# Three more raw slots for expert pieces, and a branch on TensorE that chooses between two programs that run to the end of a transformer kernel

## What is computed

```python
x = x + short_conv_mixer(rmsnorm(x), ...)            # conv
x = x + swiglu(rmsnorm(x), ...)                      # ffn1
x = x + mla_mixer(rmsnorm(x), ...)                   # mla, 8 heads
x = x + moe_swiglu(rmsnorm(x), router, ...)          # moe, 8 experts, 2 per token

x = x + fox_and_pool(rmsnorm(x), ...) @ w_out        # fox, 8 heads
x = x + memory_attention(rmsnorm(x), mem, ...)       # mem, 4 heads
x = x + swiglu(rmsnorm(x), ...)                      # ffn2
```

```python
probs = jax.nn.softmax(ht @ router)
vals, idx = lax.top_k(probs, 2)
gates = ...                                           # vals normalised, scattered to 8 columns
for e in range(8):
    out = out + gates[:, e:e + 1] * swiglu(ht, w_gate[e], w_up[e], w_down[e])
```

## Time and profile before

| | us |
|---|---|
| median of 3 runs (1244.38 to 1245.68) | 1245.11 |
| the profiled execution | 1246.09 |
| its span, first to last instruction | 1244.2 |
| TensorE busy in it | 1200.9 (97%) |
| bytes read from HBM in it | 326.26 MB |
| mean granted TensorE clock | 0.994 |

### The profile page before, as it was taken

How to read it: one execution, slowest core, us unless ns; L and a number is a source line. 1 busy time by engine, 2 the same in 40 slices (tenths; PEclk the granted TensorE clock), 3 DMA queues, 4 the chain that set the end, 5 groups by cost and what they waited for, 6 DMA issues and landing times.

```text
span 1244.2 us, 18366 instructions
## 1 busy us (share of the span) xinstructions
PE 1200.9 (97%) x7857; PEld 811.2 (65%) x7857; DVE 479.8 (39%) x710; ACT 450.0 (36%) x695; POOL 28.6 (2%) x49
## 2 busy tenths in 40 slices
PE   7999999999999999999999999988999998999998
PEld 6887888888877354436434443433688876888886
DVE  4686545546675410001001000002666664655542
ACT  6646444335775101000101100011676656444431
POOL 4000000000000000000000000010100000000000
PEclk9999999999999999999999999989999999999999
DMA  9745655553447989999999999999952450755540
GB/s 308 253 137 203 203 177 181 184 160 126 154 153 278 416 348 400 422 421 419 422 421 421 420 421 421 420 419 381 356 203 102 136 168 1 262 178 190 182 135 35
DMA packets 88019, 330.89 MB, mean 266 GB/s; under 512 B 5995, under 2 KB 13888, under 8 KB 64384
## 3 DMA queue, kind: packets, MB, share of 16 engines
q1 hardware_dynamic: 85040, 322.35, 68.3%
q0 software_dynamic: 2736, 7.27, 1.7%
q10 hardware_dynamic: 160, 0.07, 0.0%
HBM read 326.26 MB, written 3.41 MB: 265 GB/s over the span
## 4 chain that ended last, share of the span: by engine, by line
PE 86%; DMA 7%; DVE 3%; ACT 3%; issue 1%; SPq 0%; ACTq 0%; DVEq 0%
PE bank L1756 16%; PE bank L1758 16%; PE bank L1757 16%; PE bank L2108 11%; PE bank L2114 7%; PE bank L2167 7%; PE bank L2184 2%; DMA raw_beside<-in_moe_w_up 2%; DMA back<-in_moe_w_gate 2%; PE bank L2090 2%; DMA raw_over_lo<-in_moe_w_up 2%; PE bank L2204 1%; DVE w_lo L411 1%; PE bank L1851 1%; PE bank L1868 1%
## 5 line engine op out<-in xcount | busy, mean ns | idle before, releaser
L411 DVE TENSOR_TENSOR w_lo<-raw,w_hi 128x2048 fp32r<-128x2048 f32 (+3 forms) x118 | 258.0, 2200 | 169.3 <-ACT w_hi L406 169.1
L406 ACT ACTIVATE w_hi<-raw 128x2048 fp32r<-128x2048 f32 (+3 forms) x118 | 216.3, 1843 | 164.8 <-PE bank L1758 160.4
L1756 PE MATMUL bank<-w_hi,xT_hi 128*128 128x512 f32 (+2 forms) x672 | 256.8, 382 | 3.0 <-issue 1.5
L1757 PE MATMUL bank<-w_lo,xT_hi 128*128 128x512 f32 (+2 forms) x672 | 253.5, 377 | 0.0
L1758 PE MATMUL bank<-w_hi,xT_lo 128*128 128x512 f32 (+2 forms) x672 | 253.4, 377 | 0.0
L1497 DVE TENSOR_TENSOR e_act<-bank,e_act 128x512 f32<-128x512 f32 x20 | 13.8, 692 | 353.6 <-PE bank L2108 190.9
L1756 PEld LDWEIGHTS bank<-w_hi,xT_hi 128*128 128x128 f32 x672 | 127.1, 189 | 27.1 <-issue 3.7
L1758 PEld LDWEIGHTS bank<-w_hi,xT_lo 128*128 128x128 f32 x672 | 127.0, 189 | 23.0
L1757 PEld LDWEIGHTS bank<-w_lo,xT_hi 128*128 128x128 f32 x672 | 127.1, 189 | 21.7
L890 ACT ACTIVATE eT<-bank 128x512 f32<-128x512 f32 x20 | 11.5, 596 | 165.2 <-PE bank L2147 165.2
L1756 PE MATMUL bank<-w_hi,ffn_hi 128*128 128x512 f32 x176 | 68.7, 390 | 0.0
(11 more groups left out here) (428 smaller groups left out, 1415.1 us busy)
## 6 DMA issues: line engine op xcount, KB each, us to landing
raw<-in_w_gate_up SPq DMA_DIRECT2D x22, 1024.0 KB, 5.2
raw<-in_moe_w_down SPq DMA_DIRECT2D x18, 1024.0 KB, 22.1
raw_over_hi<-in_moe_w_up SPq DMA_DIRECT2D x17, 1024.0 KB, 23.4
raw_over_lo<-in_moe_w_up SPq DMA_DIRECT2D x17, 1024.0 KB, 24.2
raw<-in_moe_w_gate SPq DMA_DIRECT2D x16, 1024.0 KB, 22.0
raw_over_hi<-in_moe_w_gate SPq DMA_DIRECT2D x16, 1024.0 KB, 21.3
raw_over_lo<-in_moe_w_gate SPq DMA_DIRECT2D x16, 1024.0 KB, 22.1
raw_over_hi<-in_moe_w_down SPq DMA_DIRECT2D x16, 1024.0 KB, 19.8
```

The costliest lines, as they stand in the source:

```text
L406: nc.scalar.activation(w_hi[:, slot, :n], raw[:, slot, :n], ACT.Copy).then_inc(stream.high, 1)
L411: nc.vector.tensor_tensor(w_lo[:, slot, :n], raw[:, slot, :n], w_hi[:, slot, :n].bitcast(F32), ALU.subtract).then_inc(stream.low, 1)
L1756: mm(dst, a_hi, b_hi, start=start, stop=False)
L1757: mm(dst, a_hi, b_lo, start=False, stop=False)
```

## The change

**Slots.** EXPERT_RING becomes 19. The three new slots are a tile raw_more of 3 MB at the end of the moe region of SBUF. Room for it is made by taking two tiles out of the region: y now lies in the memory of junk (the scratch output of the squares of a norm), and moe_g, the norm's gain, in that of e_act. Piece n takes slot n % 19, and LAST_SLOTS is written anew. The first owners of the new slots (pieces 16, 17 and 18) wait for moe_product, as pieces 14 and 15 do. TensorE's use of piece n releases the issue of piece n + 19.

**Branch.** What TensorE does from the last expert to the end of the kernel becomes a function finish(over), called in both arms of a branch: finish(0) where there is no overflow, and the rounds followed by finish(1) where there is. The other engines keep their code.

```diff
-EXPERT_RING = 16
+EXPERT_RING = 19
-LAST_SLOTS = (*range(8, 16), *range(2, 8), 8, 9, 10, 11, 3, 4, 8, 9, 10, 11)
+LAST_SLOTS = (*range(16, 19), *range(2, 16), *range(16, 19), 6, 7, 8, 9)
...
+        with ExitStack() as inner:
+            y_in_junk = inner.enter_context(nc.sbuf_tensor("y_in_junk", [P, D], F32))
         junk = sb("junk", [P, T, D], mybir.dt.bfloat16)
...
-        region(back=[P, 2 * T, D], moe_g=[P, D], y=[P, D], h=[P, T, D],
+        region(back=[P, 2 * T, D], h=[P, T, D],
...
-               ahead_of=[P, T, E, E], least=[P, E, E], load=[P, 12, E])
+               ahead_of=[P, T, E, E], least=[P, E, E], load=[P, 12, E],
+               raw_more=[P, EXPERT_RING - 16, CHUNK])
+        M["y"] = y_in_junk
+        M["moe_g"] = M["e_act"][:, :, :].rearrange("p g n -> p (g n)")[:, :D]
...
-            return views + [raw_beside[:, s, :] for s in range(2)]
+            return views + [raw_beside[:, s, :] for s in range(2)] + [M["raw_more"][:, s, :] for s in range(EXPERT_RING - 16)]
...
-                pe.wait_ge(sem("moe_planned"), 1)
-                over = pe.value_load(overflow[0:1, 0:1], min_val=0, max_val=1)
-                with pe.If(over > 0):
+                def general_pass():
                     with pe.Fori(0, OVERS) as n:
...
                     light_rows()
-                pe.wait_ge(sem("moe_gT"), last_rows(over))
-                landed = landed_of(E - 1, over=over)
-                gate(landed, light_group, 2)
...
+                def finish(over):
+                    pe.wait_ge(sem("moe_gT"), last_rows(over))
+                    landed = landed_of(E - 1, over=over)
+                    gate(landed, light_group, 2)
...
+                    if "ffn2" in parts:
+                        ffn("ffn2", W2)
+                pe.wait_ge(sem("moe_planned"), 1)
+                over = pe.value_load(overflow[0:1, 0:1], min_val=0, max_val=1)
+                with pe.If(over < 1):
+                    finish(0)
+                with pe.Else():
+                    general_pass()
+                    finish(1)
```

More of the change, by code:

```diff
@@ L579, in _ @@
                 pool.wait_ge(sem("mla_nope_turned"), HEADS)
-                small(M["moe_g"][:, :], A["norm_ffn"][1:2, :].partition_broadcast(P), "moe_g")
+                small(M["moe_g"], A["norm_ffn"][1:2, :].partition_broadcast(P), "moe_g")
                 def store_rows(p):
@@ L1388, in normed @@
                 def normed(t):
-                    V.scalar_tensor_tensor(M["h"][:, t, :], x[:, t, :], rinv[:, t:t + 1], M["moe_g"][:, :],
+                    V.scalar_tensor_tensor(M["h"][:, t, :], x[:, t, :], rinv[:, t:t + 1], M["moe_g"],
                                            ALU.mult, ALU.mult).then_inc(sem("moe_h"), 1)
@@ L2426, in _ @@
-            if "mem" in parts:
-                mkv, mq = M["mkv"], M["mq"]
-                pe.wait_ge(sem("mem_kT"), MEM_HEADS // 2)
-                norm("mem", x, x_ready["mem"])
-                group(W2, start_of["mem_q"], xT_hi, xT_lo, HALF, (0, 1), "mem")
-                keep_busy(2, 9)
-                pe.wait_ge(sem("mem_q_done"), 1)
-                turn_memory(mq, "mem_queries_turned")
-                def score_m(h, to):
-                    pe.wait_ge(sem("mem_qT"), h // 2 + 1)
-                    for t in range(T):
-                        ins = mm(to[:, t * S:(t + 1) * S], M["mqT"][:, h, t * P:(t + 1) * P], M["mkT"][:, h, :],
-                                 start=True, stop=True)
-                    ins.then_inc(sem("scores_in_psum"), 1)
-                def value_m(h):
-                    if h:
-                        pe.wait_ge(sem("value_low"), before("mem", "value_low") + h)
-                    pT = M["mem_pT"][:, h % 2, :]
-                    for m in range(T):
-                        ins = mm(bank[1][:, :S], mkv[:, m, MEM + h * P:MEM + (h + 1) * P], pT[:, m * S:(m + 1) * S],
-                                 start=(m == 0), stop=(m == T - 1))
-                    ins.then_inc(sem("values_in_psum"), 1)
-                beside, around_last, rest = out_beside("mem", W2, MEM // P // 2, (), (("mem_qT", MEM_HEADS // 2),))
-                attention("mem", MEM_HEADS, [(0, P), (S, S + P), (P, S), (S + P, 2 * S)], lambda h: None, score_m, value_m,
-                          None, around_last)
-                rest()
```

290 lines of the change are left out of this document (157 added, 133 removed).

## The result

The changed kernel takes **1238.11 us** (median of 5 runs, 1237.48 to 1239.1); the kernel before, timed beside it on the same chip, 1245.24 (5 runs, 1244.38 to 1245.68). The ratio is 0.9946 with a 95% interval of 0.9934 to 0.9957: 7.1 us less forecast as 7.3, and between 5.4 and 8.2 by the interval. The profiled executions took 1238.11 and 1246.09 us, with spans of 1236.4 and 1244.2.

A forecast was written before the change was run, and what follows sets the result against it. The moe weight stream, flat at about 421 GB/s, was taken to set moe's end and all behind it. Terms: 7.4 - 0.3 + 0.5 - 0.3 = 7.3 us, from 1245.11 to 1237.8 us; range 1234.8 to 1241.5, forecast's own 1235.9 to 1239.5.

The forecast's parts named there:

- The pauses of the stream, 7.4 us: Weight stream in moe, 410 to 490 us: 382 GB/s instead of 421; three more slots close the pauses, gaining 7.4 us.
- the margin, 0.3: Slot releases near piece 42: 2.7 us of margin against 2.3 needed keeps the queue barely fed; 0.3 us lost, ends 0 and 2.1.
- Rival A: Stream, 411 to 483 us: margin too thin, pieces still in step with uses; 2.1 us lost, gain 5.5, 1239.6 us; chance 0.12.
- TensorE asks at 843.1, the pieces land at 849.0: Last two up pieces of p = 7: the transfer still arrives later, so moe's end moves by its 7.1 us, not TensorE's 10.
- The relief of the fetches, 0.5 us: End of moe: some bytes of POOL's four row fetches fall behind the last up landing, gaining 0.5 us, ends 0 and 1.7.
- piece 191: Last down piece, end of moe: it lands 7.1 to 8.6 us earlier, the new slot table closing the dip, so isn't in the way.
- The branch in moe, 0: Before p = 7: removing TensorE's 5.1 us branch stall and 2.0 of half clock gains 0, as it then waits for the transfer.
- The 1.2 us that I priced for a stall that stays: End of moe: were the branch stall and its half clock to stay, TensorE would ask at 850.2 and cost 1.2 us.
- Rival C: Branch before p = 7: a branch not taken stalls as well, costing 1.2 us, 1239.0 us; chance 0.05.
- The jump at the end, 0.3: Behind the last matmul: the moved jump costs 5.1 to 5.82 us, of which 0.2 to 0.9 show, or 0; taken as 0.3.
- Rival B: End of kernel: two jumps in a row show, TensorE ending 6.7 us past the old end; gain 0.9, 1244.2 us; chance 0.07.
- E: After TensorE's longer wait, some 6 us: low clock stays into fox; with 12 us of half-clock work 1249.8 us; chance 0.04.

The follow-up runs named there:

- second trace: The changed kernel run again, unedited, beside other runs on one chip: 1237.91 us, ratio 0.9947, length of moe 471.75 us.
- the arms swapped: The changed kernel with the branch's arms in the other order, so the way without overflow takes the far jump before p = 7: 1237.34 us, ratio 0.9943.
- the wide rows: The changed kernel with the last expert's eight down pieces read as whole 8 KB rows, not 2 KB half rows: 1238.1 us, ratio 0.9949.

## Why the prediction was right, and where it was not

**The pauses of the stream, 7.4 us, and the margin, 0.3.** Right. 410 to 490 is at 420 GB/s, and (421 - 420) x 80 / 421 = 0.2 us is what is left of a pause. The queue holds 2.6 to 2.9 us of work at its thinnest by the landings (7.4 and 7.7 us of pieces issued at 464.0 and 456.25, against 4.8 unqueued); the margin of 2.7 to 3.4 us that I worked out from the slots was this. Rival A needed 413 up to 446 and 395 from 460 to 483; both have 420. With 18 slots the thin place shows as 387.

**The gain is kept further on.** Right: the mean from 490 to 820 is 420, no slice of the page in it is under 419, and the two waits of 1.47 and 1.38 us are gone, at no gain by themselves. A third, of 0.28 us at 751.22, had been left out of the working.

**TensorE asks at 843.1, the pieces land at 849.0.** Moved by the 1.5 us of the earlier start, the trace has 842.4 (846.51 - 5.69 + 1.54) and 848.05. That it asks only 0.7 us earlier is three errors together: the 0.8 us of the register load don't show at all (the first product of p = 7 follows the last of p = 6 with no idle time), p = 6 ends 1.0 us earlier than worked out, and from there to the wait it takes 25.8 us, not 24.7, 0.78 of them the new wait at 838.88.

**The relief of the fetches, 0.5 us: the term that failed, with the step that piece 191 "moves by 7.1 to 8.6 and isn't in the way".** In the first trace the relief came up to the last up piece, and larger: that landing moved by 9.73 - 1.54 = 8.2 us, the stream's 7.1 and 1.1 of relief. But from the first transpose behind the up pieces (851.62) to the last down piece's product (870.22) it is 18.6 us; before it was 16.85 (861.52 to 878.37). The 1.75 us given back hold the two new waits, 0.49 and 0.72. So the last down piece is used 878.37 - 870.22 - 1.54 = 6.6 us earlier, not 7.6.

The second trace of the change gets to its end another way:

```profile
848.04 1.97 PE L2119 MATMUL bank<-raw_over_lo,gT 128*64 128x512 f32 x4 [5.69 <-DMA raw_beside<-in_moe_w_up]
...
862.32 1.92 PE L2209 MATMUL bank<-raw_over_hi,eT 128*64 128x512 f32 x8
```

There the last up pieces land only 6.5 us earlier (848.04, its first gate product at 406.73), less than the stream's 7.1, so no relief shows there; no down piece is waited for, and from the first transpose (853.79) to the last down product (870.74) it is 16.95 us, as before. The last down piece is used 6.0 us earlier. So how the gain is shared between the two landings is no property of the change, and in neither trace does a relief reach the end. The run without fetches fits that (5.4 us for 5.0 us of bytes).

The step on piece 191 counted on the new table to close the dip to 349 GB/s from 853 to 862. DMA share went from 0.93 to 1.02 there, but the level only from 349 to 360: the short rows hold it down, as the wide rows show (418). With them moe is 7.8 us shorter than before, and 6.0 to 6.9 in the six traces with short rows and 19 slots that have the fetches. A relief of 0 explains 0.5 us of the 1.0 missing in the first trace. The rest is less than what the change gives from one trace to the next (471.10 and 471.75) and stays open; the short rows are the nearest cause, and the timed runs with wide rows don't confirm it.

**The branch in moe, 0.** Right, and shown from both sides: the branch alone gives nothing, and the stall put back (5.88 us, or 5.80 with the arms swapped) costs nothing that the traces or the means of the timed runs show. The 1.2 us that I priced for a stall that stays did not appear either: slots alone, TensorE still waits 0.47 us for the last up pieces, since it asks at 848.9 (847.65, moved by its 1.26 us of earlier start), where I had worked out 850.2. The clock behind the last wait, priced at no change, came out so within half a microsecond: the sixteen matmuls took 5.28 us before, 5.11 and 5.75 with the change. Rival C (a branch not taken stalls as well) is out: 815.05 has no idle time.

**The jump at the end, 0.3.** Right. From the last matmul to the end of the span it takes 5.24 to 5.59 us in the eight kernels that jump there, mean 5.4, and 4.94 to 5.14 in the four that don't, mean 5.1: 0.4 us by the unrounded means. Rival B needed 6.7. This is the changed kernel's last matmul, for a span of 1236.4 (before):

```profile
1231.16 0.39 PE L1763 MATMUL bank<-w_hi,ffn_lo 128*128 128x512 f32 x1
```

The Trainium skill, in "Runtime: NRT & Kernel Launch", Instruction fetch mechanics, has a taken branch outside the fetched window stall; the 5.80 us of the jump over a whole program agree, and so does the way straight on, which shows nothing. For the short jump, 5.88 us, no row says whether its target lies outside that window. The 0.4 us at the end and the 1.78 in ffn2 would be the same kind of jump behind work that hides most of it; that is argued, not shown. The 108 ns that "Advanced Engine Details and Errata", Control Flow Timing, in the Trainium skill gives for a compare-and-branch fit none of the taken ones: the measured times decide.

**Rivals D and E.** D, that the transfers no longer bind, would have had the last up pieces used at 843.1; they are waited for, 5.69 us long. E, the clock: behind that wait 846 to 853 has a granted clock of 0.76 (0.54 in the second trace), between the levels of 1.2 and 2.4 GHz, and 853 to 862 has 1.00 again. The low stretch is over long before fox, whose part of the span didn't change (353.16 and 353.20).

**The sum.** Predicted 7.3 us off the median, measured 7.1. Off the length of moe 7.6 were predicted and 6.6 measured (6.0 in the second trace); the profiled span came out lower all the same by the 1.5 us ahead of moe, which nothing in the change accounts for. That the sum is met so closely is in part luck.

**Slips of the working.** None moves the forecast. The page's digit for the DMA share means 90% or more, not 99%, and its level is 419 to 422, with 400 in the slice up to 498 us. The relief is called "up to 1.2" and then given an upper end of 1.7. The range's lower end, with that 1.7, is 1236.0 by its own terms (1235.9 is written), and for the upper end of 1239.5 no sum is given; 7.4 - 2.1 + 0.5 - 0.3 = 5.5 makes it 1239.6.

## What to carry to other kernels

Where a stream of transfers sets the end, look for the stretch in which its level drops, and price it as (level - mean) x length / level; each further buffer was here worth about one transfer's time or a little less until the level was met; one more wasn't run. A stall of an engine that stands ahead of a wait for that stream is worth only what is left of the wait: here 5.8 us were worth 0, and the slots were the whole gain. And a longer wait can lower the clock of what follows, 1.5 to 2.2 us here. Bytes of other queues that share the engines counted in full at the end of the stage: leaving them out gave what they take. Whether moving them elsewhere would gain anything, no run here tried. Compare two traces of the same kernel before explaining a wait of half a microsecond: two of them here were gone in the second.

## What was not expected of the hardware

- A taken branch on TensorE has no one price: 5.80 to 5.88 us of idle time with its register load at the start of p = 7, near or far alike; 1.78 us idle and 2.0 to 2.8 us of time within ffn2; some 0.4 us behind the last matmul. One not taken showed no idle time, its register load neither.
- **Short rows slow down the issue as well as the transfer.** Three down pieces of the last expert in 2 KB rows, issued by SP in the changed kernel, and the same three in 8 KB rows (number: shortest/median/longest ns of one issue, first and last start us):

```profile
L396 SPq DMA_DIRECT2D raw_more<-in_moe_w_down x3: 4292/9690/12458, 819.0 to 841.5; - x3
```

```profile
L396 SPq DMA_DIRECT2D raw_more<-in_moe_w_down x3: 1992/1999/2917, 820.3 to 825.6; - x3
```

  One issue of the same megabyte took up to 12.5 us in place of 2.0, behind a queue of much the same length (the first of the three lands after 34.7 us in the changed kernel, the three after 32.6 to 33.2 with long rows). That is why piece 188 went out only at 846.10, 17 us behind the use of its slot's owner, which ended by 829.0. I had costed an issue at nothing. The queue didn't run dry by it (DMA share 1.05 and 1.02 from 846 to 862), so here it should have cost little, though the chain of the changed kernel passes through the last of these three issues (841.55, above). The slots-only kernel shows the same for these pieces, up to 12.5 us. That the number of rows waiting is what blocks an issue is how I read this pair; no run tests it by itself.
- The level of the stream was 360 GB/s with the short rows and 418 with the long ones, in the same stretch, 853 to 862 us, with the DMA engines as busy (share 1.02 and 1.01).
- Behind a wait of TensorE of 5.69 us the granted clock from 846 to 853 us was 0.76 in the changed kernel and 0.54 in its second trace; with a wait of 0.47 us (slots only) it was 1.00.
